# A two-layer decoder trunk on one core: part of the low halves of four weight units made by GpSimd, top-k rounds moved, half of one dense step moved to the next turn

## The reference

```python
for layer in range(2):
    g = norm_gains[layer]
    hn = rmsnorm(x, g[0])
    mix = window_attention(hn) if layer == 0 else dsa_sparse_attention(hn)
    x = x + rmsnorm(mix, g[1])
    hn = rmsnorm(x, g[2])
    x = x + rmsnorm(squared_relu_mlp(hn, w_up, w_down), g[3])
```

```python
logits = einsum('bthd,bsd->bths', qi_blk, ki)
score = einsum('bths,bth->bts', relu(logits), wi_blk)       # causal: -inf where key > token
_, idx = lax.top_k(score, 128)
s = einsum('bthgd,btkhd->bhgtk', q_blk, k_sel) * 64 ** -0.5  # over the 128 chosen keys
out = einsum('bhgtk,btkhd->bthgd', softmax(s), v_sel)
mix = out.reshape(512, 1024) @ w_out
```

## Time and profile before

| | |
|---|---|
| median of 3 runs | 1077.5 us (1077.49 to 1078.8) |
| the profiled execution | 1078.13 us, its span 1076.3 us |
| TensorE busy | 1056.6 us, 98% of the span |
| VectorE busy | 747.4 us, 69% |
| ScalarE busy | 538.3 us, 50% |
| GpSimd busy | 192.7 us, 18% |
| 560 to 604 us | steps 7 to 19 of the in-projection of layer 1 |
| 604 to 715 us | the turns of the attention of layer 1 |

### The profile page before, as it was taken

How to read it: one execution, slowest core, us unless ns; L and a number is a source line. 1 busy time by engine, 2 the same in 40 slices (tenths; PEclk the granted TensorE clock), 3 DMA queues, 4 the chain that set the end, 5 groups by cost and what they waited for, 6 DMA issues and landing times.

```text
span 1076.3 us, 14866 instructions
## 1 busy us (share of the span) xinstructions
PE 1056.6 (98%) x5408; PEld 859.0 (80%) x5408; DVE 747.4 (69%) x1284; ACT 538.3 (50%) x1016; POOL 192.7 (18%) x335
## 2 busy tenths in 40 slices
PE   9999999999999999999999999999999999999997
PEld 8777779888888888888778766679888888888885
DVE  5455536586697697687579898526596696696684
ACT  6677545353453443425554567645254444453422
POOL 0465320000000000005403387520000000000005
PEclk9999999999999999999999999999999999999999
DMA  9531505645545445332623333006553535535502
GB/s 294 121 79 40 118 1 119 135 88 109 101 95 118 97 99 118 90 68 51 135 43 79 79 79 79 1 1 140 116 111 85 118 81 116 117 79 118 110 9 78
DMA packets 52009, 99.94 MB, mean 93 GB/s; under 512 B 4704, under 2 KB 4832, under 8 KB 51936
## 3 DMA queue, kind: packets, MB, share of 16 engines
q1 hardware_dynamic: 51216, 98.61, 40.9%
q10 hardware_dynamic: 720, 0.38, 0.1%
HBM read 96.88 MB, written 2.10 MB: 92 GB/s over the span
## 4 chain that ended last, share of the span: by engine, by line
PE 88%; DVE 5%; DMA 3%; ACT 1%; issue 1%; SPq 1%; POOL 0%; POOLq 0%; DVEq 0%; ACTq 0%
PE bank L2038 11%; PE bank L2039 11%; PE bank L2037 11%; PE bank L2397 7%; PE bank L2398 7%; PE bank L2396 7%; PE bank L2047 6%; PE bank L2049 5%; PE bank L2048 5%; PE bank L2186 3%; PE bank L2421 3%; PE bank L2420 3%; PE bank L2422 3%; PE bank L2255 2%; DMA w_raw<-in_a_w_in 2%; PE bank L2241 2%
## 5 line engine op out<-in xcount | busy, mean ns | idle before, releaser
L2037 PE MATMUL bank<-r_hi,w_hi 128*128 128x512 f32 (+1 forms) x456 | 177.5, 389 | 0.0
L2038 PE MATMUL bank<-r_hi,w_lo 128*128 128x512 f32 (+1 forms) x456 | 177.4, 389 | 0.0
L2039 PE MATMUL bank<-r_lo,w_hi 128*128 128x512 f32 (+1 forms) x456 | 177.4, 389 | 0.0
L1636 DVE TENSOR_TENSOR w_lo<-w_raw,w_hi 128x1024 fp32r<-128x1024 f32 x84 | 102.0, 1222 | 71.3 <-ACT w_hi L1165 71.2
L1165 ACT ACTIVATE w_hi<-w_raw 128x1024 fp32r<-128x1024 f32 x84 | 87.8, 1056 | 120.2 <-PE bank L2039 82.9
L2396 PE MATMUL bank<-w_hi,hid_hi 128*128 128x512 f32 x336 | 130.7, 389 | 0.0
L2397 PE MATMUL bank<-w_lo,hid_hi 128*128 128x512 f32 x336 | 130.7, 389 | 0.0
L2398 PE MATMUL bank<-w_hi,hid_lo 128*128 128x512 f32 x336 | 130.7, 389 | 0.0
L810 POOL TENSOR_TENSOR acc<-acc,G 128x512 f32<-128x512 f32 x8 | 13.0, 1650 | 594.3 <-ACT waste L1024 594.3
L1174 ACT ACTIVATE w_hi<-w_raw,gT 128x512 fp32r<-128x512 f32 x96 | 64.5, 715 | 106.0 <-DMA w_raw<-in_w_mlp_up 74.6
L2037 PEld LDWEIGHTS bank<-r_hi,w_hi 128*128 128x128 f32 (+1 forms) x456 | 85.2, 187 | 18.2
(11 more groups left out here) (213 smaller groups left out, 2149.4 us busy)
## 6 DMA issues: line engine op xcount, KB each, us to landing
w_raw<-in_w_mlp_up SPq DMA_DIRECT2D x64, 512.0 KB, 6.5
w_raw<-in_w_mlp_down SPq DMA_DIRECT2D x64, 512.0 KB, 7.0
w_raw<-in_b_w_in SPq DMA_DIRECT2D x16, 512.0 KB, 6.8
w_raw<-in_a_w_in SPq DMA_DIRECT2D x8, 512.0 KB, 9.1
w_raw<-in_a_w_out SPq DMA_DIRECT2D x8, 512.0 KB, 5.8
w_raw<-in_b_w_out SPq DMA_DIRECT2D x8, 512.0 KB, 6.0
xt<-in_x_turned SPq DMA_DIRECT2D x8, 256.0 KB, 5.7
X<-in_x SPq DMA_DIRECT2D x4, 512.0 KB, 11.2
```

The source lines that it names most:

```text
L1636: nc.vector.tensor_tensor(half_of(w_lo[:, u % 2, :], a), b_of(PRODUCTS[i][1], a), half_of(w_hi[:, u % 2, :], a).bitcast(f32), ALU.subtract ...
L2037: nc.tensor.matmul(bank, whi, xhi, start=start, stop=False)
L2038: nc.tensor.matmul(bank, wlo, xhi, start=False, stop=False)
L2039: return nc.tensor.matmul(bank, whi, xlo, start=False, stop=stop)
```

## The change

GpSimd gets a new function, `rest_low`, that makes pieces 2 and 3 of the low parts of units 56 to 59; VectorE makes pieces 0 and 1 only. Since `rest_low` multiplies by no gain, ScalarE first writes raw x gain back in place for the two pieces (two more instructions for each unit, ahead of its third high piece) and takes the high part from there. TensorE's first step on such a unit and SyncE's load of unit u + 2 wait for both engines. On VectorE more rounds of block 2 stand ahead of the turns, 15 in place of 11, and ROUNDS_2 becomes (15, 16): one round and the mask in turn 0 and none later. TensorE runs the first two pieces of step 21 in turn 1 and the other two in turn 2 (`FILL_PARTS`).

```diff
-        {0: (0,), 1: (1,), 3: (2,), 4: (3,), ...
+        {0: (0,), 3: (2,), 4: (3,), ...
+RESCALED = (56, 57, 58, 59)
+FILL_PARTS = ({}, {1: (1, (0, 1)), 2: (1, (2, 3))})
@@ def hybrid_trunk
+        def rest_of(u):
+            return in_lo_done, 2 * RESCALED.index(u) + 2
@@ SyncE, def load(u, src)
                 sp.wait_ge(*low_of(u - 2))
+                if u - 2 in RESCALED:
+                    sp.wait_ge(*rest_of(u - 2))
@@ GpSimd
+            def rest_low(u):
+                w_h, w_l = w_place(u)
+                whole = raw(RAW[u][0])
+                for k in (2, 3):
+                    cs = slice(512 * k, 512 * k + 512)
+                    pool.wait_ge(*((w_hi_part, part_hi_no(u, 2)) if k == 2 else (w_hi_done, hi_no(u))))
+                    nc.gpsimd.tensor_tensor(w_l[:, cs], whole[:, cs], w_h[:, cs].bitcast(f32), ALU.subtract).then_inc(in_lo_done, 1)
@@
-                    for j in range(NB):
-                        rope_k(1, j)
-                    for qn in range(11, 17):
-                        rope_q(qn)
+                    rope_k(1, 0)
+                    rope_k(1, 1)
+                    rest_low(56)
+                    rope_k(1, 2)
+                    rope_k(1, 3)
+                    rest_low(57)
+                    rope_q(11)
+                    rope_q(12)
+                    rest_low(58)
+                    rope_q(13)
+                    rope_q(14)
+                    rest_low(59)
+                    rope_q(15)
+                    rope_q(16)
@@ ScalarE, def split(u), for k in range(4)
+                        if u in RESCALED and k == 2:
+                            for m in (2, 3):
+                                ms = slice(512 * m, 512 * m + 512)
+                                nc.scalar.activation(whole[:, ms], whole[:, ms], ACT.Copy,
+                                                     scale=gain(1, 0, 4 * half_no(u) + m)).then_inc(rescaled, 1)
+                        if u in RESCALED and k >= 2:
+                            act.wait_ge(rescaled, 2 * RESCALED.index(u) + k - 1)
+                            last = nc.scalar.activation(w_h[:, cs], whole[:, cs], ACT.Copy)
@@ VectorE
-            split(56)
+            split(56, (0, 1))
...
-            split(57)
+            split(57, (0, 1))
...
-            top_rounds(2, 1)
+            top_rounds(2, 3)
             q_low(1, 11)
-            top_rounds(2, 4)
-            split(58)
+            top_rounds(2, 6)
+            split(58, (0, 1))
             q_low(1, 12)
-            top_rounds(2, 6)
-            split(59)
+            top_rounds(2, 9)
+            split(59, (0, 1))
             q_low(1, 13)
-            top_rounds(2, 8)
+            top_rounds(2, 12)
             q_low(1, 14)
-            top_rounds(2, 11)
+            top_rounds(2, 15)
-            ROUNDS_2 = (11, 12, 13, 14, 15, TOPK // 8)
+            ROUNDS_2 = (15, TOPK // 8)
@@ TensorE, def in_work
                 if j == 0 and ks[0] == 0:
                     pe.wait_ge(*low_of(u))
+                    if u in RESCALED:
+                        pe.wait_ge(*rest_of(u))
@@ TensorE, def attention, in each turn behind turned(n)
+                    if n in FILL_PARTS[layer]:
+                        fill(*FILL_PARTS[layer][n])
```

More of the change, by code:

```diff
@@ L151 @@
          10: (12, 13), 11: (14, 15), 12: (16, 17), 13: (18, 19), 14: (20,), 15: (21,)},
-        {0: (0,), 1: (1,), 3: (2,), 4: (3,), 6: (4,), 7: (5,), 8: (6,), 9: (7,), 10: (8,), 11: (9,), 12: (10,), 13: (11,),
+        {0: (0,), 3: (2,), 4: (3,), 6: (4,), 7: (5,), 8: (6,), 9: (7,), 10: (8,), 11: (9,), 12: (10,), 13: (11,),
          14: (12,), 15: (13,)})
@@ L348, in hybrid_trunk @@
         w_in = [sem(f"w_in{n}") for n in range(5)]
-        w_hi_part = sem("w_hi_part")
+        w_hi_part, rescaled, in_lo_done = sem("w_hi_part"), sem("rescaled"), sem("in_lo_done")
         w_hi_done, w_lo_done, first_half_done = sem("w_hi_done"), sem("w_lo_done"), sem("first_half_done")
@@ L976, in split @@
                         cs = slice(512 * k, 512 * k + 512)
-                        last = nc.scalar.activation(w_h[:, cs], whole[:, cs], ACT.Copy,
-                                                    scale=gain(layer, 2 if name[:3] == "mlp" else 0, 4 * half_no(u) + k))
+                        if u in RESCALED and k == 2:
[6 more added lines that the diff above has]
+                            last = nc.scalar.activation(w_h[:, cs], whole[:, cs], ACT.Copy)
+                        else:
+                            last = nc.scalar.activation(w_h[:, cs], whole[:, cs], ACT.Copy,
+                                                        scale=gain(layer, 2 if name[:3] == "mlp" else 0, 4 * half_no(u) + k))
                         if u in PIECED and k < 3:
@@ L1413, in split @@
                                                               in1=w_h[:, cs].bitcast(f32), op0=ALU.mult, op1=ALU.subtract)
-                if ks[-1] == 3:
+                if ks[-1] == 3 or u in RESCALED:
                     last.then_inc(w_lo_done, 1)
```

## The result

The changed kernel takes 1082.94 us (1082.51 to 1084.01, 5 runs) where the kernel before takes 1077.5 (1077.31 to 1079.14): ratio 1.0044, 95% interval 1.0033 to 1.0055. The profiled execution took 1082.61 us, its span 1080.8, so it is 4.5 us longer than that of before (1078.13 and 1076.3). The ratio stands for 4.7 us, the two medians are 5.4 us apart; both and the 4.5 lie within the interval (3.6 to 5.9 us). The forecast of 1079.6 was too low, and so was the upper end of the range, 1082.0. The sign of the likeliest case was right.

What follows compares the result with a forecast made beforehand. TensorE, busy 98% of the span, was taken as the bound. Terms 1.6 + 0.75 + 0.1 - 0.55 = +1.9, plus 0.15, about +2.1 us on the 1077.5 median: 1079.6 us, range 1077.2 to 1082.0.

Steps and rivals of the forecast that it cites:

- the likeliest case: Whole kernel: slower by about 2.1 us, to 1079.6 us; chance 0.47.
- The chain without stalls, +0.95 us: In-projection, units 57 to 59: ScalarE's rescaling, then GpSimd's two pieces make TensorE wait, 0.95 us lost without engine stalls.
- Unit 57, +1.6 us: In-projection: late low part plus VectorE and GpSimd stalling each other, 0.5 + 0.6 + 0.5 us before unit 57.
- unit 58, +0.75: In-projection: GpSimd and VectorE's second piece meet, +0.45 us on the 0.3 without stalls.
- Unit 59, +0.1 us: In-projection: a like stall at unit 59 leaves 0.1 us beyond the delay of unit 58.
- VectorE, +0.15: VectorE's list up to query block 15: just covered, with 0.15 us added for its near miss.
- VectorE becomes the bound: Rival, units 58 and 59: GpSimd first at both, VectorE stalls, query block 15 at 609.2, total 1081.3 us; chance 0.22.
- 605.8 us for VectorE without stalls: Query block 15's low part: VectorE, losing four pieces and gaining four rounds, done at about 605.8 us; TensorE wants it at 607.3.
- The turns, -0.55 us: Turns 1 to 3: the moved half step shortens gaps, the clock stays up, transposes of turn 3 come 0.55 us earlier.
- if it does, +0.35: Turns up to turn 3: if the clock falls after all, 0.35 us lost in place of 0.55 gained.
- shift and don't shrink: Waits behind turn 3, at 633.8, 637.7 and 652.8 us: same order as before, moved in time but no shorter.
- worth nothing here: Turns 1 to 4: rounds taken out gain nothing, since up to 632 us TensorE has no wait for VectorE.

Runs made afterwards that it cites:

- e12: e5 with VectorE's own two low pieces of units 56 to 59 cut to one column; 1078.78 us, ratio 1.0007.
- e1: The kernel before with only the half of step 21 moved from turn 1 to turn 2; 1079.58 us, ratio 1.0018.
- e2: The changed kernel with step 21 back in turn 1 as one piece; low parts, rescaling and moved rounds stay; 1081.7 us, ratio 1.0034.
- e5: e2 with VectorE's rounds as they stood in the kernel before; 1080.74 us, ratio 1.0025.
- e3: The changed kernel with ScalarE's and GpSimd's work on unit 60 one turn later; 1082.18 us, ratio 1.0048.
- e9: The changed kernel with two of GpSimd's four low pieces of unit 60 one column wide; 1082.78 us, ratio 1.0037.
- e6: The kernel before with only ScalarE's rescaling of units 56 to 59 added; VectorE makes all four low pieces; 1078.07 us, ratio 1.0002.
- e11: e5 with ScalarE serving rows 2 and 3 of units 56 to 59 first; 1079.8 us, ratio 1.0011.
- e4: The kernel before with no round of block 2 in turn 0, the rest one turn later; 1076.42 us, ratio 0.9986.
- e10: The kernel before with rounds of blocks 2 and 3 put off further than in e4; 1076.48 us, ratio 0.9981.
- e7: The changed kernel with unit 60's low part made by VectorE in place of GpSimd; 1084.95 us, ratio 1.0059.

## Where the prediction held and where it failed

**The chain without stalls, +0.95 us: about right.** e12 shows 0.67 us over the in-projection of before.

**Unit 57, +1.6 us, and unit 58, +0.75: held.** Measured 1.7 us against 560 us and 0.87. The stall of 0.5 us for GpSimd in unit 57 is in the trace, and at unit 58 the engines start 0.29 us apart.

**Unit 59, +0.1 us, and VectorE, +0.15: too small.** They are 0.48 and 0.29 us. The prediction said that on its times VectorE would be ahead at both units. At unit 59 it was, by 0.07 us (596.93 and 597.00), because the added rounds had brought it there late; the two engines then met in all their pieces. Two of VectorE's four in units 58 and 59 took 1.79 us. The rival "VectorE becomes the bound" names this place and happened in part: query block 15's low part came at 608.00, 3.1 us later than in the earlier trace rows, and the transposes of turn 0 waited 0.55 us where they waited 0.29. The prediction's 605.8 us for VectorE without stalls doesn't follow from the rows it shows, which give 604.86 - 0.72 - 2.72 + 4.96 = 606.4; it needs another idle stretch of 0.63 us, before 583.75, which is in the trace but not shown.

**No lower clock in the in-projection: the term was missing.** The prediction weighed the clock in the turns, behind a wait that was there, and did not ask what a new wait of 1.6 us would do to it at 575 us. Of five profiles with the same in-projection, four show the fall and 0.65 us more. It is not in the profile of the changed kernel, so it is no part of the 4.42 us accounted for here.

**The turns, -0.55 us: the step that failed.** Measured +1.27. Two things are wrong in it. First, "if it does, +0.35" was the branch that came about, since the clock fell at 619 behind shorter waits. That branch let TensorE set the time of the transposes of turn 3 (618.05 + 6.70 = 624.75) and left ScalarE's split where it was with the clock up. The moved half of the step ran at the lower clock, behind a wait of 0.33 us for VectorE's masked scores, so the split that its signal releases came 3.26 us later than before, counted from the transposes of turn 0, not 2.05 (e1, with the clock up there, has 2.06). Turn 3 then waited 0.94 us for GpSimd, and the stretch up to it costs +0.71. Second, the account ended at turn 3. It said that the waits behind "shift and don't shrink". They grew: GpSimd is busy for nearly all of the 33 us from 624 to 657, so the 3.31 us for which it stands at 621 to 624, waiting for that split, come back as waits at turns 3, 5 and 6 (2.66 us together). e1 shows the loss with nothing else changed, -0.48 us to turn 3 and +2.08 behind it, but there it is VectorE's list that carries it. The changed kernel has fewer rounds in the turns; its VectorE stands 3.91 us for the same exponentials and has the time.

**The rounds taken out of turns 1 to 4, "worth nothing here": not contradicted.** e2 and e5 differ in the rounds alone. VectorE is busy 39.7 us from 615 to 665 in e2, and 45.6 in e5, with those rounds; turns 0 to 5 take 32.61 and 31.42 us. No gain is seen, but the clock is down twice as long in e2, so the two profiles don't show a price of nothing either.

**The sum.** In-projection +3.35 where +2.6 was predicted, turns +1.27 where -0.55 was. The turns are the larger error, 1.8 us against 0.75.

**What stays open.** Why the clock falls at 619 in the changed kernel and not in e3 and e9, whose waits there are much the same (1.29 and 0.80 us; 1.27 and 0.80), isn't explained by any row. Neither e3 nor e9 settles in time that GpSimd's list alone makes the waits of turns 5 and 6 in the changed kernel; only the traces say so. And what the moved half step costs within the changed kernel is not shown in time: the ratios of the changed kernel and of e2, 1.0044 and 1.0034, have overlapping intervals.

## What to carry to other kernels

When a step is moved, follow the engine that its signal releases, and the engines that this one releases, until each next has idle time: a hole of 2 to 3 us comes back through whichever list has no slack, ten to twenty microseconds later (VectorE's in e1, GpSimd's in the changed kernel). Work shared out between VectorE and GpSimd, both reading SBUF, is not work saved; price it with the pair's time side by side, and count what stands behind both. And allow for each added wait that the clock may fall behind it: on this kernel one such fall is worth about 1.6 us, as much as the wait itself, and it comes in some executions and not in others.

## What the runs showed of the hardware

- Turns 0 to 5 take 31.4 us (31.21 to 31.46) in five kernels without the moved step whose waits there stand in different places (before, e5, e6, e11, e12), and each has one stretch at the lower clock, between 617 and 641. e4 and e10, which have no such stretch, take 29.99 and 29.71. With the moved step the waits for GpSimd are longer, and a clock that stays up is no sign of a short stretch: e3 and e9 have no fall in the turns and take 31.99 and 31.46.
- Each fall stands behind a wait: at 577 behind 1.87 us (e2), at 634 behind 1.63 (e1), at 631 behind 2.40 (e7), and it lasts about 3.4 us each time (a mean of 0.66 over 5 us is 3.4 us at 0.50). In e2's turns it lasts twice as long, and the execution is 1.4 us above its kernel's median. But the length of the wait doesn't decide it: there is no fall behind 1.88 us at 575 in the changed kernel, behind 1.87 at 576 in e5 or behind 1.57 and 2.18 in the turns of e3.
- A stall between VectorE and GpSimd lasts for what is left of the instruction that came first: 0.5 us for GpSimd beside a piece of 0.75, 1.04 for VectorE beside one of 1.28, 2.0 for GpSimd beside one of 2.26. The Trainium skill, SBUF — State Buffer, section "Who interferes with whom", calls the pair of ports that the two share an exclusive lock, with the order of issue deciding who blocks. These rows agree; what they add is that a longer VectorE instruction, though less than half as long as GpSimd's for the same data, makes the stall longer.
